# Handing over a ring of gathered expert rows row by row instead of in groups of four

## The reference

```python
q = (xb @ w_q)                                   # 8 heads, 2 halves
s1, i1 = top_k(s[:, :, 0], 16); s2, i2 = top_k(s[:, :, 1], 16)
sc, ci = top_k(s1 + s2 over all pairs, 16)       # 16 of 16384 experts for each head
g = softmax(sc)
act = gelu(einsum('td,thkd->thk', xb, u_tab[eidx]))
y   = einsum('thk,thkd->td', g * act, v_tab[eidx])
```

## Time and profile before

| | us |
|---|---|
| median of three runs | 3981.04 |
| profiled execution, its own time | 3993.61 |
| profiled execution, span | 3991.7 |
| PE busy (share of the span) | 3233.3 (81%) |
| DVE busy | 2688.8 (67%) |
| POOL busy | 1529.7 (38%) |
| ACT busy | 405.1 (10%) |

### The profile page before, as it was taken

One profiled execution on the slowest core, in us unless ns is written; L12 is line 12 of the kernel. 1 busy time (PEld: TensorE's weight loads), 2 busy tenths in 40 slices (PEclk: granted clock), 3 DMA queues, 4 the chain that ended last, 5 costly groups with the idle time before them and its releaser, 6 DMA issues.

```text
span 3991.7 us, 54562 instructions
## 1 busy us (share of the span) xinstructions
PE 3233.3 (81%) x17422; PEld 2044.7 (51%) x17422; DVE 2688.8 (67%) x5879; ACT 405.1 (10%) x955; POOL 1529.7 (38%) x1447
## 2 busy tenths in 40 slices
PE   7948885994498899888888899962888898898876
PEld 3522122593355555555554684952555565565543
DVE  3787655189877788877666322579677787776566
ACT  1111111111111000000000100111111000000000
POOL 1446650010055555555444000010455554555443
PEclk9969997996699999999999899985999999999998
DMA  4678873221199999999999327120799999999987
GB/s 145 221 253 317 298 276 71 100 86 69 53 360 346 344 361 357 357 358 352 341 341 341 129 85 122 43 85 27 270 351 346 344 368 339 355 342 333 340 325 282
DMA packets 299181, 1021.19 MB, mean 256 GB/s; under 512 B 57805, under 2 KB 58229, under 8 KB 295870
## 3 DMA queue, kind: packets, MB, share of 16 engines
q0 software_dynamic: 188928, 687.95, 47.1%
q1 hardware_dynamic: 84928, 324.07, 21.7%
q10 hardware_dynamic: 25214, 7.72, 2.1%
HBM read 1013.90 MB, written 5.72 MB: 255 GB/s over the span
## 4 chain that ended last, share of the span: by engine, by line
DVE 32%; DMA 26%; PE 21%; issue 10%; POOL 8%; ACT 1%; DVEq 1%; POOLq 0%; SPq 0%; ACTq 0%
DMA area<-peer_v_in,area 7%; DVE area L1752 6%; POOL area L570 6%; DMA hn<-peer_u_in,area 6%; DMA area<-peer_u_in,area 5%; DVE xs L1760 5%; DVE hn L1760 5%; PE ps L652 4%; PE ps L815 4%; PE ps L664 4%; DMA hn<-peer_v_in,area 4%; DMA area<-cache_k_in,area 3%; PE ps L737 3%; DVE hn L1752 2%; PE ps L827 1%
## 5 line engine op out<-in xcount | busy, mean ns | idle before, releaser
L922 PE MATMUL ps<-area 128*128 128x512 f32 x2048 | 991.5, 629 | 74.1 <-DVE area L1740 74.0
L913 PE MATMUL ps<-hT,area 128*128 128x256 f32 x4096 | 946.1, 385 | 107.5 <-DMA area<-peer_ut_in 106.6
L913 PEld LDWEIGHTS ps<-hT,area 128*128 128x128 f32 x4096 | 778.8, 192 | 358.6 <-issue 261.3
L570 POOL DMA_INDIRECT area<-peer_u_in,area x396 | 444.6, 1123 | 1131.0 <-DVEq L1762 690.7
L570 POOL DMA_INDIRECT area<-peer_v_in,area x396 | 420.5, 1062 | 625.3 <-DVEq L1762 450.9
L922 PEld LDWEIGHTS ps<-area 128*128 128x128 f32 x2048 | 389.0, 199 | 491.5 <-issue 490.4
L1752 DVE CUSTOM_DVE_ANT_0 area<-area,hn 128x1024 f32<-128x1024 f32 x384 | 450.4, 1222 | 211.2 <-DMA hn<-peer_u_in,area 109.9
L854 PE MATMUL ps<-area 128*128 128x32 bf16 x6144 | 196.5, 180 | 287.6 <-DVE area L1645 286.1
L1760 DVE SCALAR_TENSOR_TENSOR xs<-area,xs 128x1024 f32<-128x1024 f32 x192 | 247.0, 1286 | 228.6 <-DMA area<-peer_v_in,area 149.0
L854 PEld LDWEIGHTS ps<-area 128*128 128x128 bf16 x6144 | 183.2, 99 | 344.2 <-issue 331.8
L652 PE MATMUL ps<-area,hT 128*128 128x512 f32 (+1 forms) x560 | 249.7, 607 | 43.4 <-DVEq L1508 36.8
(11 more groups left out here) (261 smaller groups left out, 3072.4 us busy)
## 6 DMA issues: line engine op xcount, KB each, us to landing
area<-peer_ut_in SPq DMA_DIRECT2D x256, 512.0 KB
area<-peer_v_in SPq DMA_DIRECT2D x256, 512.0 KB
area<-wq_in SPq DMA_DIRECT2D x8, 2048.0 KB, 19.0
area<-w_in_c_in SPq DMA_DIRECT2D x6, 2048.0 KB, 7.6
area<-w_in_a_in SPq DMA_DIRECT2D x5, 2048.0 KB, 11.4
area<-peer_u_in,area POOLq DMA_INDIRECT x396
area<-peer_v_in,area POOLq DMA_INDIRECT x396
area<-w_out_a_in SPq DMA_DIRECT2D x2, 2048.0 KB, 10.5
```

Of the source, the lines that this page charges most:

```text
L570: pool.indirect_dma_start(ring[r], None, ins[what + str(l)], bass.IndirectOffsetOnAxis(ap=idx[:, i:i + 1], axis=0)).then_inc(rows_landed[h ...
L913: m = pe.matmul(ps[c % 2][:, 0:DT * P], us[c][:, k, :], hT[:, k, 0:DT * P], start=(k == 0), stop=(k == KD - 1))
L922: m = pe.matmul(ps[2 + 2 * t + h][:, :], cT[:, c % 2, t * P:(t + 1) * P], vs[c % 2][:, h * 512:(h + 1) * 512], start=False, stop=False, sk ...
```

## The change

The ring keeps its eight slots. Each slot gets its own landing semaphore, and `row_groups_free` becomes `rows_free`, which counts single rows. GpSimd waits before each gather, VectorE waits before each row and frees it at once. In the dots ranges the dot product itself increments `rows_free`, so that nothing waits for the last of four; before the 16 results of a loop trip are copied out, VectorE waits for the count instead. In the values ranges each row gets an increment and a wait of its own.

```diff
-    row_groups_free = sem("row_groups_free")
-    rows_landed = [sem(f"rows_landed{i}") for i in range(2)]
+    rows_free = sem("rows_free")
+    rows_landed = [sem(f"rows_landed{i}") for i in range(GSLOTS)]
...
-        def group(l, what, idx, half):
+        def group(l, what, idx, half, free):
             for i in range(GRP):
                 r = half * GRP + i
+                wait_apart(pool, go, rows_free, free(i))
                 pool.indirect_dma_start(ring[r], None, ins[what + str(l)],
-                                        bass.IndirectOffsetOnAxis(ap=idx[:, i:i + 1], axis=0)).then_inc(rows_landed[half], 16)
+                                        bass.IndirectOffsetOnAxis(ap=idx[:, i:i + 1], axis=0)).then_inc(rows_landed[r], 16)
...
-                    wait_apart(pool, go, row_groups_free, i * (GBODY // GRP) + (g0 + n + 1))
                     pool.wait_ge(pool_steps, n // 2 + 1)
-                    group(l, what, ixs[:, n * GRP:(n + 1) * GRP], n % 2)
+                    group(l, what, ixs[:, n * GRP:(n + 1) * GRP], n % 2,
+                          lambda q: i * GBODY + ((g0 + n) * GRP + q + 1))
...
             for k in range(DK):
-                if k % GRP == 0:
-                    pe.wait_ge(rows_landed[k // GRP], 64 * (l * (GROUPS // 2) + 2))
+                pe.wait_ge(rows_landed[k], 16 * (l * (GROUPS // 2) + 2))
...
-                if k % GRP == GRP - 1:
-                    m.then_inc(row_groups_free, 1)
+                m.then_inc(rows_free, 1)
...
             for k in range(DK):
-                if k % GRP == 0:
-                    dve.wait_ge(rows_landed[k // GRP], 64 * (l * (GROUPS // 2) + 1))
+                dve.wait_ge(rows_landed[k], 16 * (l * (GROUPS // 2) + 1))
...
-                if k % GRP == GRP - 1:
-                    dve.sem_inc(row_groups_free, 1)
+                dve.sem_inc(rows_free, 1)
...
-                        wait_apart(dve, go, rows_landed[half], j * 128 + 64 * (base + c // 2 + 1))
                         for i in range(GRP):
                             row, q = ring[half * GRP + i], c * GRP + i
+                            wait_apart(dve, go, rows_landed[half * GRP + i], j * 32 + 16 * (base + c // 2 + 1))
                             if not values:
                                 m = dve.tensor_tensor_reduce(row, row, hn[:, t, :], 1.0, 0.0, ALU.mult, ALU.add,
                                                              d16[:, q:q + 1])
-                                if i < GRP - 1:
-                                    m.then_inc(dve_steps, 1)
-                                    step.n += 1
-                                else:
-                                    step(m)
+                                m.then_inc(rows_free, 1)
                             else:
                                 step(dve.scalar_tensor_tensor(acc[i % 2], row, d16[:, q:q + 1], acc[i % 2],
                                                               ALU.mult, ALU.add))
-                        dve.sem_inc(row_groups_free, 1)
+                                dve.sem_inc(rows_free, 1)
                     if not values:
+                        done = (l * GROUPS + DG + r * (SEL // GRP)) * GRP + GSLOTS
+                        wait_apart(dve, go, rows_free, j * GBODY + (done + GBODY))
                         step(dve.tensor_copy(dots[:, bass.ds(j * GBODY, GBODY)], d16[:, :]))
```

More of the change, by code:

```diff
@@ L594, in _ @@
                 for half in range(2):
-                    pool.wait_ge(row_groups_free, base + 2 * n + half + 1)
-                    group(l, what, dix[:, half * GRP:(half + 1) * GRP], half)
+                    group(l, what, dix[:, half * GRP:(half + 1) * GRP], half,
+                          lambda i: (base + 2 * n + half) * GRP + i + 1)
             for t in reversed(range(GT)):
@@ L894, in peer @@
                                   start=(k == 0), stop=(k == DK - 1))
-                if k % GRP == GRP - 1:
-                    m.then_inc(row_groups_free, 1)
-            pe.wait_ge(row_groups_free, l * GROUPS + DG + 2)
+                m.then_inc(rows_free, 1)
+            pe.wait_ge(rows_free, (l * GROUPS + DG + 2) * GRP)
             pe.sem_inc(dve_bank_full, 2)
@@ L1300, in _ @@
         dve.sem_inc(value_slots_free, len(vpages) - 1)
-        dve.sem_inc(row_groups_free, 2)
+        dve.sem_inc(rows_free, GSLOTS)
         dve.sem_inc(coefs_ready, 2)
```

## The result

| kernel | runs | median us | ratio to before, 95% interval |
|---|---|---|---|
| before | 4 | 3983.4 | |
| after | 4 | 3821.1 (3819.4 to 3831.1) | 0.9594 [0.9567, 0.9621] |

The change makes the kernel 162 us faster. The forecast was 91 us, 3890; the time lies 8 us under rival A's 3829. The profiled execution took 3820.58 us, with a span of 3818.8 us, 172.9 us less than before. Of the executions of the kernel before that ran beside the experiments, one took 8582.1 us at a granted clock of 0.402; no ratio here uses it.

The account below looks back on a forecast made before the run. The prediction took the circle of row release, descriptors, flight and VectorE work as the bound, with DMA rate next. Terms -99 and +8 sum to -91 us: 3981 to 3890 us, own range 3850 to 3930, 8-in-10 range 3815 to 4005.

Parts of the forecast that it names:

- rival A: Fuller ring: DMA engines hold 375 GB/s, six ranges gain 155 us, 3829 us in all; chance 0.14.
- The circle that bound the kernel before: Ring: VectorE's release, GpSimd's descriptors, flight and VectorE's work take 9.1 us a chunk; after the change 5.9, no longer the bound.
- What is late next: After the ring's waits go, the data itself is late: the DMA engines' rate, taken as 362 GB/s, bounds the gain.
- the largest term: Six ranges other than the values ranges with gates: 1726.0 us to 1627 us at 362 GB/s, -99 us.
- VectorE in the values ranges: Three added handovers a chunk cost 0.30 us each; VectorE bounds the values ranges with gates, +8 us in all.
- The 5 us of remaining landing waits: Values ranges with gates: some landing waits stay, 5 us added within the +8 us.
- VectorE in the dots ranges: Added waits run under dot products; the 12.1 us a range stall ahead of L1740 goes; not the bound, counted 0.
- GpSimd: Descriptor writes: 1024 waits replace 256, up to 1.4 us more a chunk, staying under 8.4 us and hidden in the flight.
- D: Dots ranges: descriptor writes slowed beside dot products make GpSimd the bound, +29 us there, 3989 us in all; chance 0.08.
- B: No room: DMA engines already give their average 345 GB/s, longer queues only lengthen flights; 3989 us; chance 0.12.
- The HBM figure: All six ranges: the skill's 358 GB/s would give -80 us instead of -99; doubted as a hard limit.
- C: All values ranges: VectorE becomes the bound, +115 us, 4096 us, or near 4040 if dots ranges gain; chance 0.10.

Follow-up runs that it names:

- e1: Changed kernel, but VectorE waits for all four rows of a half ahead of the first; rows still freed one by one: 3817.8 us, ratio 0.9590.
- e2: Changed kernel, but GpSimd starts on a half only when all its four rows are free: 3853.1 us, ratio 0.9685.
- e4: Kernel before the change, with u chunks issued earlier by the same edit as e3: 3979.3 us, ratio 0.9984.
- e3: Changed kernel, with SyncE issuing u of chunk n+2 behind v of chunk n, instead of u of n+1: 3705.8 us, ratio 0.9307.
- e7: Changed kernel with the edits of e3 and e5 together: 3639.6 us, ratio 0.9141.
- e6: Changed kernel with two more waits, both already met, ahead of each accumulation in the values ranges: 3899.8 us, ratio 0.9798.
- e5: Changed kernel; in values ranges the accumulation itself increments rows_free and VectorE waits for the one before last: 3764.7 us, ratio 0.9463.

## Why the prediction was right, and where it was off

**The circle that bound the kernel before: right.** The landing waits went: 211.2 us ahead of the dot products became 4.7, and what is left ahead of the accumulations is no landing. The chain lost GpSimd. e1, e2 and e4 agree. The working named two losses of slack, slots that lie free and rows that lie landed. Only the first was worth having by itself to the full: e1 keeps all of the gain without the second.

**What is late next: wrong, and with it the size of the largest term.** The step "the gain is bounded by their rate" took the DMA engines as the next bound, and 362 GB/s as what they do, read from stretches of a kernel that was not bound by them. The ranges after ran at 361 to 403 GB/s, 375 over the six (589.1 MB in 1571.8 us), which is by chance the rate of the best 80 us of the earlier trace rows. e3 and e7 show 396 to 410 GB/s over whole ranges. A rate from a stretch of the profile is what was asked of the engines there, not what they can do. The term was -99 and measured -154.2 us. Rival A's 3829 us is the closest number for the same reason and by the same luck: it took 375 GB/s as what the engines hold, and they were not the bound. "SyncE and its table loads are not touched" was true of the edit and missed that their circle was next. What was needed stood in the trace before: TensorE busy for 254 us of a range, and on the page 106.6 us of idle time ahead of L913 for the u table, a wait that the working left out. TensorE's work plus its waits for u nearly fills a dots range after: 252.9 us busy and 23.6 us of waits of 278.4 us. That the measured time still lies inside the stated range of 3815 to 4005 us, if below the forecast's own 3850 to 3930, is owed to the width of that range and not to this step.

**VectorE in the values ranges: right in kind, too dear.** The handover costs 0.22 us, not 0.30: the wait has the same value for the four rows of a half, so no register is computed between (the added instructions are one increment and one wait). The forecast's own working with 0.22 gives 8.06 + 0.66 = 8.72 us a chunk, and the ranges take 8.73 and 8.77 us (279.5 / 32, 280.5 / 32). That VectorE bounds these and not the last ranges is confirmed by e6, and by e3, which left the first of them at 278.4 us. The 5 us of remaining landing waits did not appear.

**VectorE in the dots ranges: right.** The stall of 12.1 us a range ahead of L1740 after a dot product is gone, and the added waits are hidden: VectorE now waits for gelu there. That the lost stall doesn't move the time fits this and no run shows it alone.

**GpSimd: right.** Over all eight slots the mean descriptor write went from 1.17 to 1.26 us for a u row and from 1.06 to 1.23 us for a v row. (The rows and after show 1.12 and 1.34 us for u, but they hold six of the eight slots; in the two others it fell, 1.30 to 1.01 us.) GpSimd is busy 5.1 to 5.4 us a chunk and waits for rows the rest. D and B didn't happen. The Trainium skill ("SBUF — State Buffer", section "Who interferes with whom") says that a VectorE instruction with two SBUF inputs contends with a GpSimd instruction that reads SBUF. The longer means agree with that, but no run isolates it, and it stayed off the path.

**The HBM figure.** The ranges of e7 move 396 to 410 GB/s. The Trainium skill ("SBUF — State Buffer", section "A bandwidth-pool intuition that's wrong (but worth ruling out)") gives about 358 GB/s for HBM to one core, as half of what a stack gives. Here the measurement decides: it was no limit, with one core running.

**Slips in the sums.** They change nothing in the forecast. The shortest chunk is 8.8 us by the division given (281.7 / 32). Of the -99, the dots ranges' part is -64 and the last ranges' -35 by the earlier trace rows at 362 GB/s, not -70 and -29; rival D comes to 3983 us with that, and C with gaining dots ranges to 4032 us, not 4040.

## What to carry to other kernels

A ring that is freed in groups makes the descriptor writes of a whole group part of its circle; free slots one by one, and ask only then whether waiting one by one brings anything (here it didn't). When a circle is taken away, the next bound can be another circle and not a resource, as here: look for every load that is issued behind a wait for something later than its own slot. And if an engine must release something after each operation, let the operation do it and wait for the one before last, so that no operation stands behind a full stop (e5: 56 us).

## What was not expected of the hardware

Accumulations of 128x1024 fp32 with no stop between them start 1.20 us apart and last 1.28 us each in the profile, so they overlap (e5); with a wait for the one before they start 1.32 us apart, and with an increment and one more wait 1.54 us. The DMA engines of one core held 409 or 410 GB/s for 245.9, 247.5 and 233.2 us (e7), with 4 KB pieces from two queues, a third of the bytes from tables read in order and the rest gathered.
